# Scores of a chunkwise recurrence by groups of 32 key columns instead of 128, in a three-block kernel on one Trainium2 core

## What is computed

```python
def step(state, inp):                       # over chunks of 64 tokens
    qc, kc, gc, vc = inp                    # gc: log of the forget gate f
    b = jnp.cumsum(gc, axis=2)
    diff = b[:, :, :, None, :] - b[:, :, None, :, :]
    decay = jnp.where(causal, jnp.exp(jnp.minimum(diff, 0.0)), 0.0)
    scores = jnp.einsum('bhtk,bhtsk,bhsk->bhts', qc, decay, kc)
    o = einsum(qc * exp(b), state) + einsum(scores, vc)
    ...                                     # state decays and takes in kc, vc
```

## Time and profile before

| | |
|---|---|
| median of three runs | 965.92 us |
| span of the profiled execution | 963.2 us (its own time outside the profile is not recorded) |
| PE busy | 952.3 us, 99% |
| DVE busy | 748.2 us, 78% |
| ACT busy | 547.7 us, 57% |
| POOL busy | 89.4 us, 9% |
| granted TensorE clock, mean | 0.999 |
| DMA | 166.62 MB, mean 173 GB/s |

### The profile page before, as it was taken

The page is one execution under the profiler, slowest core; times in us unless marked ns, Lnnn a source line. Parts: engine busy times, 40 slices in busy tenths (PEclk is TensorE's granted clock), DMA queues, the critical chain, the costliest instruction groups (busy, mean ns, idle before and its releaser), DMA issues.

```text
span 963.2 us, 18430 instructions
## 1 busy us (share of the span) xinstructions
PE 952.3 (99%) x7530; PEld 909.1 (94%) x7530; DVE 748.2 (78%) x1129; ACT 547.7 (57%) x819; POOL 89.4 (9%) x91
## 2 busy tenths in 40 slices
PE   9999999999999999999999999999999999999998
PEld 8999999999999998999999999999999999999998
DVE  6998778978855599867987844489887998787777
ACT  6652366656454476756665544455666665556455
POOL 5334101000201000001000201001001000000000
PEclk9999999999999999999999999999999999999999
DMA  8733444766666836436476575626636467665651
GB/s 256 243 120 115 143 128 140 218 200 197 195 183 193 267 109 197 150 113 183 136 215 197 176 214 184 194 68 182 183 110 202 127 197 214 187 190 170 203 175 44
DMA packets 164723, 166.62 MB, mean 173 GB/s; under 512 B 6784, under 2 KB 162832, under 8 KB 164640
## 3 DMA queue, kind: packets, MB, share of 16 engines
q1 hardware_dynamic: 162752, 163.47, 55.5%
q0 software_dynamic: 1056, 1.19, 0.5%
q10 hardware_dynamic: 832, 0.79, 0.4%
HBM read 163.82 MB, written 1.08 MB: 171 GB/s over the span
## 4 chain that ended last, share of the span: by engine, by line
PE 82%; DVE 12%; issue 2%; ACT 2%; DMA 2%; SPq 0%; POOL 0%; ACTq 0%; DVEq 0%
PE ps L657 19%; PE ps L660 16%; PE ps L649 13%; DVE w_lo L1990 4%; PE ps L676 3%; PE ps L677 3%; PE ps L678 3%; PE ps L682 2%; PE ps L683 2%; PE ps L684 2%; PE ps L689 2%; PE ps L609 2%; PE ps L617 2%; PE ps L690 2%; PE ps L691 2%
## 5 line engine op out<-in xcount | busy, mean ns | idle before, releaser
L1990 DVE TENSOR_TENSOR w_lo<-w_raw,w_hi 128x1024 fp32r<-128x1024 f32 (+4 forms) x314 | 375.0, 1205 | 116.1 <-ACT w_hi L1424 110.3
L1424 ACT ACTIVATE w_hi<-w_raw 128x1024 fp32r<-128x1024 f32 x298 | 313.3, 1056 | 200.3 <-PE ps L660 47.6
L657 PE MATMUL ps<-xs,w_hi 128*128 128x256 f32 x1012 | 132.6, 277 | 0.0
L657 PEld LDWEIGHTS ps<-xs,w_hi 128*128 128x128 f32 x1012 | 127.0, 188 | 4.5
L660 PE MATMUL ps<-xs,w_lo 128*128 128x256 f32 x832 | 112.2, 277 | 0.0
L660 PEld LDWEIGHTS ps<-xs,w_lo 128*128 128x128 f32 x832 | 102.9, 188 | 0.2
L682 PE MATMUL ps<-xs,w_hi 128*128 128x256 f32 x320 | 91.4, 285 | 0.4 <-DVE w_lo L1990 0.4
L683 PE MATMUL ps<-xs,w_hi 128*128 128x256 f32 x320 | 89.3, 279 | 0.0
L684 PE MATMUL ps<-xs,w_lo 128*128 128x256 f32 x320 | 89.3, 279 | 0.0
L649 PE MATMUL ps<-xs,w_hi 128*128 128x512 f32 x326 | 85.1, 393 | 0.3 <-DVE mo L2018 0.2
L1431 ACT ACTIVATE tmp<-ps 128x512 f32<-128x512 f32 x75 | 44.5, 593 | 70.6 <-PE ps L649 62.6
(11 more groups left out here) (431 smaller groups left out, 1896.6 us busy)
## 6 DMA issues: line engine op xcount, KB each, us to landing
w_raw<-in_mlp_w_up SPq DMA_DIRECT2D x64, 512.0 KB, 4.2
w_raw<-in_mlp_w_down SPq DMA_DIRECT2D x64, 512.0 KB, 3.5
w_raw<-in_a_w_in SPq DMA_DIRECT2D x32, 512.0 KB, 4.3
w_raw<-in_w_gate SPq DMA_DIRECT2D x22, 512.0 KB, 3.8
w_raw<-in_w_up SPq DMA_DIRECT2D x22, 512.0 KB, 4.6
w_raw<-in_w_down SPq DMA_DIRECT2D x20, 512.0 KB, 4.4
w_raw<-in_w_kv SPq DMA_DIRECT2D x16, 512.0 KB, 4.3
w_raw<-in_w_in SPq DMA_DIRECT2D x16, 512.0 KB, 3.9
```

The lines of the kernel that those rows point to most:

```text
L657: mm(ps[:, 2 * pset + n, at], hi[:, kk, n * P:(n + 1) * P], x[:, kt0 + kk, at], start=False, stop=False)
L1424: o = fn(dst, raw, ACT.Copy)
L1990: return v.tensor_tensor(d, x, y, ALU.subtract)
```

## The change

The uses of levels up to 16 no longer load 128 keys. For each group of 32 tokens (`SUB`), 32 key columns are loaded, and the result goes to the 32 partitions of that group. Each of these five uses now covers all four heads with 32 matmuls (8 tiles of 128 tokens, 4 groups each): 32 query columns at the first two, 16 at the next three. The four groups of a tile follow one another, on four different sets of partitions. The two double steps become single uses, so a quad has eight uses instead of ten; levels 32, 64 and `cross` are as before, and each level stays in its step of the loop.

DVE takes the small results into a compact `acc_sub` [128, 16, 32] with smaller masks: 256 elements of a partition at use 0, 128 and 128 at use 1, 128 at uses 2 to 4. ACT spreads `acc_sub` into `acc` with four copies of 32 partitions by 256 elements for each quad (`spread_sub`), at q = 20 and q = 25, and PE's `head_outputs` waits for it (`acc_spread`). POOL clears `acc_sub` at the start. The mask table has 464 columns fewer, and the arena behind it is moved by 64 bytes more.

```diff
+SUB = 32
+SUBS = P // SUB
...
-T_ODD = T_LEVEL + P
-T_BLOCK = T_ODD + CHUNK
-LEVELS = 6
-T_FREQ = T_BLOCK + LEVELS * CHUNK
+T_ODD = T_LEVEL + SUB
+T_BLOCK = T_ODD + SUB // 2
+LEVELS = 4
+T_FREQ = T_BLOCK + LEVELS * SUB // 2
...
-FIRST_STEP, QUAD_STEPS, QUAD_USES = 10, 8, 10
-
-
-def uses_of(n):
-    quad, j = divmod(n, QUAD_STEPS)
-    return [QUAD_USES * quad + u for u in (((0, 1), (2, 3))[j] if j < 2 else (j + 2,))]
+FIRST_STEP, QUAD_STEPS, QUAD_USES = 10, 8, 8
...
+        top[0] += HALF_PERIOD
...
+        acc_sub = over("acc_sub", [P, 2 * HEADS, SUB], F32, 8 * K8 + 5120)
...
-                elif u == 2:
-                    pe.wait_ge(k_decayed, 7 * quad + 1)
-                    pe.wait_ge(q_decayed, 7 * quad + 1)
-                    pe.wait_ge(q_moved, quad + 1)
-                elif u > 3:
-                    pe.wait_ge(k_decayed, 7 * quad + u - 2)
-                    pe.wait_ge(q_decayed, 7 * quad + u - 2)
+                else:
+                    pe.wait_ge(k_decayed, 7 * quad + u)
+                    pe.wait_ge(q_decayed, 7 * quad + u)
+                    if u == 1:
+                        pe.wait_ge(q_moved, quad + 1)
                 if u == QUAD_USES - 1:
                     for hh in range(4):
                         hd = 4 * quad + hh
                         o = mm(ps[:, bank, hh * P:(hh + 1) * P], hk[:, hd, 0:P], hqd[:, hd, P:S], start=True, stop=True)
-                elif u < 4:
-                    for hh in range(2):
-                        hd = 4 * quad + 2 * (u % 2) + hh
-                        for tile in range(2):
-                            at = (2 * hh + tile) * P
-                            o_ap = ps[:, bank, at:at + P]
-                            if u < 2:
-                                rhs = both_q(hd, tile * P, [[HEADS * S + 1, 2], [2, CHUNK]])
+                elif u < 5:
+                    b = 2 ** u
+                    n_q = SUB if u < 2 else SUB // 2
+                    for c in range(8):
+                        hd = 4 * quad + c // 2
+                        for g in range(SUBS):
+                            at = c % 2 * P + SUB * g
+                            o_ap = ps[SUB * g:SUB * (g + 1), bank, n_q * c:n_q * (c + 1)]
+                            if u == 0:
+                                rhs = both_q(hd, at, [[HEADS * S + 1, 2], [2, SUB // 2]])
                                 o_ap = o_ap.rearrange("p (a s) -> p s a", s=2)
+                            elif u == 1:
+                                rhs = both_q(hd, at + 2, [[HEADS * S, 2], [4, SUB // 4], [1, 2]])
+                                o_ap = o_ap.rearrange("p (x g j) -> p x g j", x=2, j=2)
                             else:
-                                rhs = both_q(hd, tile * P + 2, [[HEADS * S, 2], [4, P // 4], [1, 2]])
-                                o_ap = o_ap.rearrange("p (g x j) -> p x g j", x=2, j=2)
-                            o = mm(o_ap, hk[:, hd, tile * P:(tile + 1) * P], rhs, start=True, stop=True)
-                elif u > 6:
-                    b = 2 ** (u - 2)
+                                rhs = hqd[:, hd, at:at + SUB].rearrange("p (g s b) -> p g s b", s=2, b=b)[:, :, 1, :]
+                                o_ap = o_ap.rearrange("p (g b) -> p g b", b=b)
+                            o = mm(o_ap, hk[:, hd, at:at + SUB], rhs, start=True, stop=True)
+                else:
+                    b = 2 ** u
                     for hh in range(4):
                         hd = 4 * quad + hh
                         for tile in range(2):
@@ -925,20 +928,12 @@
                                 key = tile * P + 2 * b * g
                                 o = mm(ps[2 * b * g:2 * b * g + b, bank, at + b * g:at + b * (g + 1)], hk[:, hd, key:key + b],
                                        hqd[:, hd, key + b:key + 2 * b], start=True, stop=True)
-                else:
-                    b = 2 ** (u - 2)
-                    for hh in range(4):
-                        hd = 4 * quad + hh
-                        for tile in range(2):
-                            at = (2 * hh + tile) * CHUNK
-                            rhs = hqd[:, hd, tile * P:(tile + 1) * P].rearrange("p (g s b) -> p g s b", s=2, b=b)[:, :, 1, :]
-                            o_ap = ps[:, bank, at:at + CHUNK].rearrange("p (g b) -> p g b", b=b)
-                            o = mm(o_ap, hk[:, hd, tile * P:(tile + 1) * P], rhs, start=True, stop=True)
                 o.then_inc(lvl_scored, 1)
...
+                pe.wait_ge(acc_spread, quad + 1)
...
-                    for n in uses_of(q - FIRST_STEP):
-                        use(n)
+                    use(q - FIRST_STEP)
...
+            def spread_sub(quad):
+                heads, subs = slice(4 * quad, 4 * quad + 4), slice(8 * quad, 8 * quad + 8)
+                if quad == 0:
+                    act.wait_ge(acc_zero, 2)
+                act.wait_ge(lvl_taken, QUAD_USES * quad + 5)
+                for g in range(SUBS):
+                    own = slice(SUB * g, SUB * (g + 1))
+                    o = fn(acc[own, heads, :].rearrange("p h (m t) -> p (h m) t", m=2)[:, :, own], acc_sub[own, subs, :],
+                           ACT.Copy)
+                o.then_inc(acc_spread, 1)
...
+                elif q in (20, 25):
+                    spread_sub(q // 25)
...
+                dve.wait_ge(lvl_scored, n + 1)
                 if u == 0:
-                    dve.wait_ge(lvl_scored, n + 2)
                     raw = hq[:, heads, :].rearrange("p h t -> p (h t)").rearrange("p (g s) -> p g s", s=4)
                     v.tensor_copy(raw[:, :, 2], raw[:, :, 1]).then_inc(q_moved, 1)
-                    decay_q(quad, 1)
-                elif u == 2:
-                    dve.wait_ge(lvl_scored, n + 2)
-                    dve.wait_ge(f_blocks, 6 * quad + 1)
-                    decay_q(quad, 2)
-                else:
-                    dve.wait_ge(lvl_scored, n + 1)
+                elif u < QUAD_USES - 1:
+                    dve.wait_ge(f_blocks, 6 * quad + u)
+                if u < QUAD_USES - 1:
+                    decay_q(quad, 2 ** u)
                 wait(dve, lvl_taken, n)
                 if u == QUAD_USES - 1:
                     v.tensor_copy(cross[:, heads, :], ps[:, bank, :].rearrange("p (h t) -> p h t", h=4)).then_inc(lvl_taken, 1)
                     return
-                if u < 4:
-                    two = slice(4 * quad + 2 * (u % 2), 4 * quad + 2 * (u % 2) + 2)
-                    whole = acc[:, two, :].rearrange("p h t -> p (h t)")
-                    if u < 2:
-                        mask = table[:, T_LEVEL:T_LEVEL + P].bitcast(U32).rearrange("p (a t) -> p a t", a=1).broadcast_to([P, 4, P])
-                        v.copy_predicated(whole.rearrange("p (c t) -> p c t", c=4), mask,
-                                          ps[:, bank, :].rearrange("p (c t) -> p c t", c=4)).then_inc(lvl_taken, 1)
-                        return
-                    src = ps[:, bank, :].rearrange("p (c g x j) -> p c g x j", c=4, x=2, j=2)
-                    odd = whole.rearrange("p (c g j s) -> p c g j s", c=4, j=2, s=2)[:, :, :, :, 1]
-                    upper = whole.rearrange("p (c g s j) -> p c g s j", c=4, s=2, j=2)[:, :, :, 1, :]
-                    mask = [table[:, at:at + CHUNK].bitcast(U32).rearrange("p (a g j) -> p a g j", a=1, j=2)
-                            .broadcast_to([P, 4, CHUNK // 2, 2]) for at in (T_ODD, T_BLOCK)]
-                    link(v.copy_predicated(odd, mask[0], src[:, :, :, 0, :]))
-                    v.copy_predicated(upper, mask[1], src[:, :, :, 1, :]).then_inc(lvl_taken, 1)
-                    return
-                b = 2 ** (u - 2)
-                at = T_BLOCK + (u - 3) * CHUNK
-                whole = acc[:, heads, :].rearrange("p h t -> p (h t)")
-                dst = whole.rearrange("p (c g s b) -> p c g s b", c=8, s=2, b=b)[:, :, :, 1, :]
-                src = ps[:, bank, :].rearrange("p (c g b) -> p c g b", c=8, b=b)
-                if u > 6:
-                    dve.wait_ge(f_blocks, 6 * quad + u - 2)
-                    decay_q(quad, b)
+                if u > 4:
+                    b = 2 ** u
+                    whole = acc[:, heads, :].rearrange("p h t -> p (h t)")
+                    dst = whole.rearrange("p (c g s b) -> p c g s b", c=8, s=2, b=b)[:, :, :, 1, :]
+                    src = ps[:, bank, :].rearrange("p (c g b) -> p c g b", c=8, b=b)
                     for g in range(CHUNK // b):
                         keys_ = slice(2 * b * g, 2 * b * g + b)
                         o = v.tensor_copy(dst[keys_, :, g, :], src[keys_, :, g, :])
                     o.then_inc(lvl_taken, 1)
                     return
-                mask = table[:, at:at + CHUNK].bitcast(U32).rearrange("p (a g b) -> p a g b", a=1, b=b)\
-                    .broadcast_to([P, 8, CHUNK // b, b])
-                dve.wait_ge(f_blocks, 6 * quad + u - 2)
-                decay_q(quad, b)
```

(44 more changed lines are left out.)

## The result

The changed kernel takes 955.5 us (median of four runs, 955.04 to 955.81) against 965.75 for the kernel before on the same chip. The ratio is 0.9896, with a 95% interval from 0.9882 to 0.991. The forecast was 956.2 us, in a range from 954.6 to 962.3. The span went from 963.2 to 953.6 us.

The account below looks back on a forecast made before the run. PE's in-order stream was taken as the bound nearly everywhere, DVE at the first quad's start. Quads winning 4.83 + 4.86 = 9.7 us, off 965.9, gave 956.2 us, range 954.6 to 962.3.

Parts of the forecast that it names:

- PE's new price: Each changed score use on PE costs 0.82 us, from 1.81 or 1.78, saving 4.86 us for a quad.
- The counts of the earlier trace: At level 32 two more weight loads than matmuls under way, at level 64 one more: taken to fit two independent chains.
- The bound of "at least half of 0.0675": Rival on PE: neighbouring groups do not overlap, at least 0.034 us a record, 2.4 us a use; 971 us, chance 0.05.
- The floor of 25 ns: Rival on PE: start-to-start never below about 25 ns, 1.8 us a use, nothing won there; 965.0 us, chance 0.04.
- The start: First quad, DVE-bound: use 1 at 47.0 instead of 47.76, 0.76 us won, a stall of 1.3 us for 0.88.
- The first quad behind it: After use 1, steps take 3.65 us instead of 4.6; the first quad wins 4.83 us in all.
- The margin called 0.15 at use 4: First quad: DVE has the queries ready at 57.8 us and PE wants them at 57.95.
- The walk: DVE's work followed through the first quad's steps, leaving margins of 0.15 to 0.7 us before PE wants its operands.
- The second quad: Second four heads: the uses win 4.86 us; POOL's margin of 1.26 us is used up but not overdrawn.
- Edits at nothing: ACT's spread, POOL's clearing of `acc_sub` and the smaller table DMA were said to cost nothing.
- its cover: ACT's 1.7 us spread stands behind a weight rounding, ahead of a 3.59 us gap, 2.6 in future, so nothing waits.
- The rest of the kernel: Behind the stage, PE's own progress releases everything, so the stage's gain should arrive at the end in full.

Follow-up runs that it names:

- the three orders: Changed kernel with its 32 matmuls a use reordered: one set at a time 966.86 us, alternating sets two apart 959.05 us, alternating neighbouring sets 959.19 us.
- changed_again: The changed kernel profiled again with nothing altered, as partner of other runs: 955.81 us; 57.1 us for the stage, 854.4 us behind it.
- changed_third: The changed kernel profiled a third time with nothing altered, as partner of other runs: 955.94 us; 57.9 us for the stage, 854.7 us behind it.
- the three versions tried: Changed kernel with later DVE `w_lo` halves and key factors 956.53 us; that plus earlier POOL gate products 958.82 us; earlier products alone 956.74 us.

## Why the prediction was right

- **PE's new price.** It was taken as 0.82 us and measured 0.86 to 0.89, on the ground named: independent sets of 32 partitions, as the three orders show. The step was a little too good. It gave 64 records on four sets the 0.62 us of level 32's 32 records on two; they take 0.66 to 0.70, mostly as the later records of a use slow down. The ten uses won about 0.5 us less than reckoned. The counts of the earlier trace rows were weak support for it: they come from the opening of a use, and the ends of matmuls are modelled in the profile. The bound of "at least half of 0.0675" for a record alone on its set was too high as well: it is 0.029 with the edges of the use.
- **The floor of 25 ns.** The Trainium skill, "TensorE: Matmul & The Clock Gate", section "Wait — 56ns, not 53.3ns?", would have left nothing of the gain. Across four sets records follow at 0.70 / 64 = 0.011 us, so it does not hold there. On one set they follow at 0.025 to 0.028 inside a use, which fits it, and that kernel indeed won nothing. The Trainium skill's "TensorEngine Tiling (Array Packing)", in its table of theoretical speedups, gives up to 4 times for a dimension of 32; 2.6 was measured over a whole use.
- **The start.** Use 1 was expected at 47.0 and came at 47.38, 0.36 of it from the later start of the stage; the stall was 1.16 us, for 1.3. POOL, the held-up `w_lo` and the quick copy came as walked through.
- **The first quad behind it.** The margin called 0.15 at use 4 failed by 0.23 us; the others held. 4.6 us were won, for 4.83. The walk followed DVE alone, and what failed came from elsewhere: a weight half landed late, ScalarE rounded it before it turned to the keys, and DVE waited for those. The first pair of rows is the changed kernel, the second `changed_again`, where the half landed earlier and use 4 did not wait (in `changed_third` DVE waited 0.90 us there and use 4 0.32):

```profile
49.00 1.06 ACT L1418 ACTIVATE w_hi<-w_raw 128x1024 fp32r<-128x1024 f32 x1 [3.27 <-DMA w_raw<-in_a_w_in]
52.03 1.99 DVE L2278 TENSOR_SCALAR hk<-hk,small 128x256 f32<-128x256 f32 x4 [0.73 <-ACT hk L1570]
```

```profile
48.02 1.06 ACT L1418 ACTIVATE w_hi<-w_raw 128x1024 fp32r<-128x1024 f32 x1 [1.77 <-DMA w_raw<-in_a_w_in]
51.07 2.09 DVE L2278 TENSOR_SCALAR hk<-hk,small 128x256 f32<-128x256 f32 x4
```

- **The second quad.** 5.2 us, for 4.86, although its uses cost 0.05 more each. Most of the rest is the projections' records between them: five quanta there ran at 0.113 to 0.114 us a record, where four of these five had 0.118 in the kernel before. From 81.90 to 84.39 us are 22 records, 0.113 each; 24 x 0.0045 is 0.1 us a quantum, about 0.4 in all. The prediction had no such term, and what decides between the two paces is open.
- **Luck in the sum.** The stage won 9.8 us, for 9.7. That is closer than the steps were: 0.5 us less from the uses and 0.2 at the margin were made up by the quicker quanta, which nobody had reckoned with.
- **Edits at nothing.** The spread is free, by its cover, as said. The row of the 64 bytes was missing: the prediction spoke of the table's smaller DMA and not of its length, which would have moved every operand behind it. The number came out right because the change itself undoes that move.
- **The rest of the kernel** passed the gain on: 853.5 and 853.3 us behind the stage.

## What to carry to other kernels

Small score matmuls are priced by how many sets of 32 output partitions take turns: the same work cost 2.04, 1.25 or 0.88 us on one, two or four sets, so order them so that neighbours in the stream go to different sets. When PE gets faster inside a handed-over recurrence, walk the other queues: here the next bounds are DVE's order, the lock with GpSimd and GpSimd's products, and in the three versions tried moving one only fed the next. And when a table changes its length, look where the matmul operands behind it begin.

## What the runs showed that was not expected

A moving operand in the arena, 64 bytes off its place within 128, costs up to 0.120 us a record of 256 columns instead of 0.113, which is 10 to 11 us in this kernel, in the changed one and in the one before alike.

The place is not all. The quanta of the projections, whose operands `xs`, `w_hi` and `w_lo` lie ahead of the arena, showed two paces in the same kernel, 0.113 and 0.118, each nearly constant within a quantum, with `xs` as the moving operand and with the weights. The same quantum can have either from one execution to the next: the one behind use 0 ran at 0.118 in the changed kernel's profile and at 0.113 in `changed_again`. So the place of the operands alone does not decide it; the cause was not tried.
